# Where the preparation of a state-space layer stands among the matmuls: turns, powers and tables of eight blocks at other places

## The reference

```python
x = x + 0.5 * swiglu(rms_norm(x, g[0]), ffn_w_in[0, 0], ffn_w_out[0, 0])   # x @ w_in, silu(gate) * up, @ w_out
h = rms_norm(x, g[1])
lam_bar = jnp.exp(lam * step)
b_bar = ((lam_bar - 1.0) / lam)[..., None] * b
# x_t = lam_bar x_{t-1} + b_bar u_t,  y_t = Re(C x_t) + D u_t, by group
x = x + s5_mixer(h, ...)
```

## Time and profile before

| | |
|---|---|
| median of three runs | 1791.58 us (1790.89 to 1791.99) |
| profiled execution, its own time | 1792.96 us |
| its span, first to last instruction | 1791.1 us |
| mean granted clock of TensorE | 0.995 |
| TensorE busy | 1753.7 us, 98% of the span |
| VectorE, ScalarE, POOL busy | 928.5, 652.6, 324.7 us |

### The profile page before, as it was taken

One profiled execution on the slowest core, in us unless ns is written; L12 is line 12 of the kernel. 1 busy time (PEld: TensorE's weight loads), 2 busy tenths in 40 slices (PEclk: granted clock), 3 DMA queues, 4 the chain that ended last, 5 costly groups with the idle time before them and its releaser, 6 DMA issues.

```text
span 1791.1 us, 22436 instructions
## 1 busy us (share of the span) xinstructions
PE 1753.7 (98%) x8598; PEld 1435.5 (80%) x8598; DVE 928.5 (52%) x1067; ACT 652.6 (36%) x897; POOL 324.7 (18%) x276
## 2 busy tenths in 40 slices
PE   9999899997999999999999999999999999999998
PEld 6787787876788888888888888888777888888887
DVE  7768978648555344433374334333674544444333
ACT  6332233347434333332253333322474433333222
POOL 8997533016014000000000000000200200000000
PEclk9999999999999999999999999999999999999999
DMA  5364645588433332333223332333310333322321
GB/s 200 118 165 123 182 133 157 156 301 311 143 102 96 95 94 95 100 98 94 94 83 107 103 95 94 95 101 99 96 46 1 107 106 100 97 94 94 97 91 47
DMA packets 80788, 206.50 MB, mean 115 GB/s; under 512 B 24048, under 2 KB 34416, under 8 KB 79696
## 3 DMA queue, kind: packets, MB, share of 16 engines
q1 hardware_dynamic: 69664, 189.86, 33.6%
q0 software_dynamic: 2592, 13.51, 2.2%
q10 hardware_dynamic: 8464, 2.20, 0.5%
HBM read 182.46 MB, written 23.07 MB: 115 GB/s over the span
## 4 chain that ended last, share of the span: by engine, by line
PE 83%; DVE 6%; ACT 3%; POOL 3%; DMA 2%; issue 2%; ACTq 0%; SPq 0%; DVEq 0%; POOLq 0%
PE bank L1628 26%; PE bank L1630 26%; PE bank L1629 26%; DVE w_split L1179 2%; ACT w_split L761 1%; DMA op_slot<-s_ops 1%; PE bank L1979 1%; PE bank L1958 1%; ACT x_gained L792 0%; DVE ops_out L1228 0%; DVE up L1223 0%; ACTq L794 0%; DVE gate L1222 0%; DVE ops_out L1225 0%; DVE ops_out L1224 0%
## 5 line engine op out<-in xcount | busy, mean ns | idle before, releaser
L1179 DVE TENSOR_TENSOR w_split<-w_raw,w_split 128x1024 fp32r<-128x1024 f32 x296 | 402.9, 1365 | 624.4 <-ACT w_split L761 623.7
L1628 PE MATMUL bank<-h_split,w_split 128*128 128x512 f32 x1504 | 589.1, 392 | 2.4 <-DVE gate L1191 0.9
L1630 PE MATMUL bank<-h_split,w_split 128*128 128x512 f32 x1504 | 585.4, 389 | 0.0
L1629 PE MATMUL bank<-h_split,w_split 128*128 128x512 f32 x1504 | 585.2, 389 | 0.0
L761 ACT ACTIVATE w_split<-w_raw 128x1024 fp32r<-128x1024 f32 x296 | 312.2, 1058 | 642.5 <-PE bank L1630 634.2
L1628 PE MATMUL bank<-g_split,w_split 128*128 128x512 f32 (+1 forms) x854 | 330.4, 387 | 8.5 <-DVE w_split L1179 4.9
L1628 PEld LDWEIGHTS bank<-h_split,w_split 128*128 128x128 f32 x1504 | 282.3, 188 | 65.3 <-DVE h_split L1198 2.0
L1629 PEld LDWEIGHTS bank<-h_split,w_split 128*128 128x128 f32 x1504 | 282.4, 188 | 59.1 <-issue 1.2
L1630 PEld LDWEIGHTS bank<-h_split,w_split 128*128 128x128 f32 x1504 | 282.3, 188 | 58.9
L1629 PE MATMUL bank<-g_split,w_split 128*128 128x512 f32 (+1 forms) x854 | 329.3, 386 | 0.0
L1630 PE MATMUL bank<-g_split,w_split 128*128 128x512 f32 (+1 forms) x854 | 329.2, 385 | 0.0
(11 more groups left out here) (298 smaller groups left out, 1154.0 us busy)
## 6 DMA issues: line engine op xcount, KB each, us to landing
w_raw<-wstream SPq DMA_DIRECT2D x296, 512.0 KB, 3.5
op_slot<-s_ops SPq DMA_DIRECT2D x5, 2048.0 KB, 13.5
s_ops<-ops_out SPq DMA_DIRECT2D x16, 512.0 KB, 3.0
op_slot<-s_ops POOLq DMA_DIRECT2D x3, 2048.0 KB, 14.1
s_ops<-c_pow POOLq DMA_DIRECT2D x8, 512.0 KB, 5.2
s_ops<-k_window SPq DMA_DIRECT2D x64, 64.0 KB, 3.3
x_res<-xT SPq DMA_DIRECT2D x8, 256.0 KB, 6.2
s_u<-x_gained ACTq DMA_DIRECT2D x8, 256.0 KB, 7.6
```

The costliest lines, as they stand in the source:

```text
L1179: tt(W[:, r, 1, :], RAW[:, r, :], W[:, r, 0, :].bitcast(F32), ALU.subtract).then_inc(s_lo, 1)
L1628: mm(bank, hi, x_hi, start=start, stop=True, skip_group_check=True)
L1629: mm(bank, hi, x_lo, start=False, stop=True, skip_group_check=True)
L1630: return mm(bank, lo, x_hi, start=False, stop=True, skip_group_check=True)
```

## The change

Nothing is added or removed but waits: the same operations stand at other places. Turns: block 0 goes from input tile 4 to 5 of part one, 3 from output tile 2 to 3, 4 from output tile 5 of part one to input tile 1 of part two, 5 from input tile 2 to 3, 7 from 8 to 7; blocks 1, 2 and 6 stay. The taps follow one tile behind. Tables: blocks 0 and 1 go from output tiles 0 and 1 of part one to 2 and 5, block 2 from output tile 4 to input tile 0 of part two, 3 from input tile 1 to 3, 4 from 4 to 6, 5 from 6 to 7, 7 from 10 to 9; block 6 stays at 8. One wait is added on POOL: the powers of blocks 3 and later start when the low half of part one's last gate is written. Two calls of `s5_ops` are added, since none stood at input tiles 0 (VectorE) and 1 (TensorE).

```diff
--- before.py
+++ after.py
@@ -80,12 +80,12 @@
 
 IN, OUT = range(2)
 S5_STAGES = (FFN0A1, FFN0A2)
-TURN_AT = {(FFN0A1, IN, 4): 0, (FFN0A1, IN, 7): 1, (FFN0A1, IN, 9): 2, (FFN0A1, OUT, 2): 3, (FFN0A1, OUT, 5): 4,
-           (FFN0A2, IN, 2): 5, (FFN0A2, IN, 5): 6, (FFN0A2, IN, 8): 7}
-TAPS_AT = {(FFN0A1, IN, 5): 0, (FFN0A1, IN, 8): 1, (FFN0A1, IN, 10): 2, (FFN0A1, OUT, 3): 3, (FFN0A1, OUT, 6): 4,
-           (FFN0A2, IN, 3): 5, (FFN0A2, IN, 6): 6, (FFN0A2, IN, 9): 7}
-TABLES_AT = {(FFN0A1, OUT, 0): 0, (FFN0A1, OUT, 1): 1, (FFN0A1, OUT, 4): 2, (FFN0A2, IN, 1): 3, (FFN0A2, IN, 4): 4,
-             (FFN0A2, IN, 6): 5, (FFN0A2, IN, 8): 6, (FFN0A2, IN, 10): 7}
+TURN_AT = {(FFN0A1, IN, 5): 0, (FFN0A1, IN, 7): 1, (FFN0A1, IN, 9): 2, (FFN0A1, OUT, 3): 3, (FFN0A2, IN, 1): 4,
+           (FFN0A2, IN, 3): 5, (FFN0A2, IN, 5): 6, (FFN0A2, IN, 7): 7}
+TAPS_AT = {(FFN0A1, IN, 6): 0, (FFN0A1, IN, 8): 1, (FFN0A1, IN, 10): 2, (FFN0A1, OUT, 4): 3, (FFN0A2, IN, 2): 4,
+           (FFN0A2, IN, 4): 5, (FFN0A2, IN, 6): 6, (FFN0A2, IN, 8): 7}
+TABLES_AT = {(FFN0A1, OUT, 2): 0, (FFN0A1, OUT, 5): 1, (FFN0A2, IN, 0): 2, (FFN0A2, IN, 3): 3, (FFN0A2, IN, 6): 4,
+             (FFN0A2, IN, 7): 5, (FFN0A2, IN, 8): 6, (FFN0A2, IN, 9): 7}
 
 N_IN0A, N_S5, N_IN0B, N_KV, N_LAT, N_DQ, N_IN1B, N_FINAL = range(8)
 
@@ -652,6 +652,7 @@
             powers(tt, link, PA, 7, t1, t2)
             nc.gpsimd.memset(TM[:, 0:8], 0.0).then_inc(s_near, 1)
             pool.wait_ge(s_near, 1)
+            pool.wait_ge(s_g_lo, HALF)
             for k in range(3, BLOCKS):
                 make_powers(k)
 
@@ -1271,6 +1272,8 @@
                     dve.wait_ge(s_rstd, n + 1)
                 gated(stage, 0, 0, stage + 2)
                 split(stage, 3)
+                if stage == FFN0A2:
+                    s5_ops(stage, IN, 0)
                 ffn_in_loop(stage)
 
             def add_ffn(stage, d):
@@ -1726,6 +1729,8 @@
                 in_tile(stage, 1, 1, base, src, within=within)
                 if after:
                     after()
+                if stage == FFN0A2:
+                    s5_ops(stage, IN, 1)
                 if stage not in S5_STAGES:
                     in_turns(pe, stage, ffn_in_turn)
                     return
```

## The result

The changed kernel takes 1796.09 us (median of 17 runs, 1792.25 to 1796.67) against 1792.01 of the kernel before on the same chip (17 runs, 1789.62 to 1795.15): a ratio of 1.0015, 95% interval 1.0009 to 1.0022. It is slower by 2.7 us by the ratio (4.1 by the medians), where 1783 was forecast; both the range and the likeliest case are missed.

The account below looks back on a forecast made before the run. TensorE was taken as the bound (83% of the chain), its four waits and lowered clock costing 16.35 us; less new waits and clock of 1.0, 1.5, 3.3 and 1.8, 8.75 is gained: 1783 us, range 1776 to 1790.

Parts of the forecast that it names:

- Turn 0, and part one's last gate: Part one: TensorE's waits of 2.21 us ahead of turn 0 and 3.15 in output tile 0 go, with 1.8 of clock.
- Tables 0 beside powers 4: Part one's output tiles: tables 0 run wholly beside powers 4; the 4.91 us wait shrinks to 1.0 (0 to 2).
- The last gate of part two: First output tile of part two: a new wait of 3.3 us (1.9 to 5) for tile 10's gate, with 1.8 of clock.
- The next two iterations repeat what the trace shows: Part two, VectorE after turn 4: unchanged until iteration 3, which starts 26.7 us behind the end of input tile 1.
- TensorE wants them behind tiles 4 and 5 and turns 5 and 6: Part two: banks wanted 25.0 us after input tile 3, free at 26.2; a wait of 1.5 (0 to 4), without clock.
- Turn 1: Part one: POOL's step into block 1's c_pow may start some us later, and turn 1 has two tiles for it.
- The sum: Whole kernel: 16.35 - 1.0 - 1.5 - 3.3 - 1.8 = 8.75 us gained, 1784.2 for the profiled execution.
- The signs of being wrong: Tables 0 ending before 175, no operation of tables 3 held, or the last wait outside 1.9 to 5 us.
- the signs listed for the forecast: No wait at turn 0 or part one's first output tile; tables 0 at 12 us or more; gate waits 1.5 and 3.3.
- The case slower than before: Rival, part two: longer VectorE backlog makes the last gate 13.7 us late, with 5 of clock; 1796.5; 5%.
- Full blocking: Rival, part two: each POOL operation in iteration 3 holds VectorE for its whole length; a wait of 6 us; 1790; 18%.

Follow-up runs that it names:

- experiment 4: The changed kernel without POOL's added wait for part one's last gate: 1800.46 us, ratio 1.0058 to the kernel before.
- experiment 2: The changed kernel with part two's turns 4 to 7 at input tiles 1, 4, 7, 9, taps and tables moved to suit: 1789.23 us, ratio 0.9983 to the kernel before.
- experiment 10: The changed kernel with tables 3 at input tile 4 and tables 7 at input tile 10 of part two: 1782.55 us, ratio 0.9947 to the kernel before.
- experiment 9: The changed kernel with POOL's powers of blocks 5 to 7 done for the first channel group only: 1782.26 us, ratio 0.9941 to the kernel before.
- experiment 3: The changed kernel with tables 7 behind part two's last gate, at input tile 10 for 9: 1789.04 us, ratio 0.9991 to the kernel before.
- experiment 1: The changed kernel with ScalarE's copies of a turned block ahead of the next input tile's gate in part two: 1792.01 us, ratio 1.0004 to the kernel before.
- experiment 7: The kernel with turns three tiles apart in part two, with tables 0 moved to input tile 9 of part one: 1789.06 us, ratio 0.9978 to the kernel before.
- experiment 8: The changed kernel with SyncE's load of the last u ahead of operator loads 4 and 5: 1794.74 us, ratio 1.0013 to the kernel before.

## Why the prediction was wrong, step by step

- **Turn 0, and part one's last gate: right.** Both waits are gone and the clock is 1.00 there; experiment 4 brings the second back, and costs 7.7 us by the ratios and 5.3 by the medians, where 3.15 + 1.8 was the term.
- **Tables 0 beside powers 4: right in kind, the wait smaller.** They run from 168.51 to 184.5, 15.9 us (15.35 was taken). The low half behind them was forecast 1.0 us late (0 to 2); it was on time, while in experiments 2 and 10 it was 1.1 late.
- **The last gate of part two: right.** 3.3 us and 1.8 of clock were forecast, 2.98 and 1.9 came. Experiment 9 gives 3.00 with POOL all but silent, so it is the plain addition of VectorE's operations that the term was worked out as; experiment 3 removes it by moving the one set of tables.
- **"The next two iterations repeat what the trace shows": right, and it hid the failure.** Iteration 3 was to start 26.7 us behind turn 4's place and did at 27.2 (247.32); the banks were to be free 26.2 us behind turn 5 and were 26.9 (273.35, against turn 5's start at 246.49; that start was itself 2.94 late, so from the end of tile 3, the E3 of the prediction, it is 29.8). Experiment 1 shows the case that the prediction reckoned with, a turn 5 that does not wait: iteration 3 and tables 3 are held by 8.0 us where 8.1 was taken, the banks are free at E3 + 27.0, and TensorE waits 1.96 where 1.5 was taken. The stretch of VectorE's operations was thus sized well. Its rows in experiment 1, turn 5 on TensorE and then VectorE's iteration 3, tables 3 and the gate behind them:

```profile
243.75 0.63 PE L1707 MATMUL bank<-c_pow,b_pow 128*16 128x128 f32 x16
...
247.84 1.21 DVE L1183 TENSOR_TENSOR w_split<-w_raw,w_split 128x1024 fp32r<-128x1024 f32 x1
...
266.77 0.68 DVE L1232 TENSOR_TENSOR ops_out<-ops_out,up 128x512 f32<-128x512 f32 x1
...
270.01 0.69 DVE L1195 TENSOR_TENSOR gate<-gate,bank 128x512 f32<-128x512 f32 x1 [0.70 <-ACT gate L768]
```

  The step that failed is the one behind it: "TensorE wants them behind tiles 4 and 5 and turns 5 and 6". What TensorE wanted first was turn 6, and a turn waits for ScalarE's copies of the block before, 4 us further down ScalarE's order than the gate's second operation. For a turn the sum held no wait but POOL's. Where it had 1.5 us without clock, 2.94 + 6.25 came, with 4.4 of clock. A smaller miss lies beside it: no term had a gate wait behind powers 7, and experiment 1, where no turn of part two waits, has 3.16 us there.
- **It could be read before.** ScalarE's timeline before, behind turn 5 at 246.43, three tiles ahead of turn 6:

```profile
266.66 0.63 ACT L767 ACTIVATE gate<-gate 128x512 f32<-128x512 f32 x1 [6.50 <-DVE gate L1189]
268.58 1.04 ACT L761 ACTIVATE w_split<-w_raw 128x1024 fp32r<-128x1024 f32 x1
...
271.09 1.09 ACT L814 ACTIVATE ops_out<-bank 128x512 f32<-128x512 f32 x2
```

  The copies end at 272.18, 25.75 us behind the turn that they copy. Three tiles and a turn are 34.3 us, two are 23.37. Two tiles apart the next turn waits 2.4 us if VectorE is as late as it was here, beside powers 6, and not later; 2.94 came. With those powers cut to one group in eight the copies end by 22.5 (experiment 9), and nothing waits. For turn 6 the stretched tables stand ahead of that gate as well.
- **Turn 1: missed for the same reason.** Turn 0 moved from three tiles ahead of turn 1 to two, and 1.14 us of wait for the copies of block 0 came. All ten experiments leave this place as the change has it, and of the eleven profiled executions five have the wait, at 1.14 to 1.18 us, and six none: the margin is near zero.
- **The sum.** Forecast were 7.6 us of waits and clock left of 16.35; 19.6 are there. The difference, 12.0, is the gap between the forecast for the profiled execution, 1784.2, and its 1796.6, but for 0.4.
- **The signs of being wrong.** None of the three came true: tables 0 ended at 184.5, operations of tables 3 were held, and the last wait was 2.98. They tested the terms that the sum had, and none looked at a turn. Of the signs listed for the forecast only the wait of 1.5 us for a gate near input tile 6 is missing.
- **The rivals.** The case slower than before came out with its time (1796.5) and not with its mechanism, so that its time is luck: the last gate was to be late by 13.7 and was by 2.98. Full blocking (1790) put its 6 us on the same gate of part two as the forecast; its rule, that of the Trainium skill, "SBUF — State Buffer", section "SBUF: two separate sides", says that a VectorE operation with both inputs in SBUF and a POOL operation that reads SBUF shut each other out. The trace agrees in kind (3.3 and 3.6 us for operations of 1.1, and experiment 9's low halves of 1.232 against 1.610 mean), but not in the size that the rival drew from it: tables 3 took 12.1 us, with three of six operations held, and in experiment 1 iteration 3 and tables 3 together were held by the 8.0 us named above, where the rival took six times 2.2, or 13.2.

From the last addition of part two to the end experiments 2 and 7 seem to need 2 us less than the others (1389.3 and 1389.0, against 1390.3 to 1391.9). They do not: from the end of TensorE's matmuls of part two they need 1392.2 us, the others 1390.6 to 1392.2. In these two the last addition comes 2.92 and 3.24 us behind that, against 0.27 to 0.31 in all others, and TensorE's waits of 2.58 and 2.90 us for ScalarE's square stand there. Not settled is what makes VectorE late at that place.

## What to carry to other kernels

When an operation is moved nearer to its predecessor, list everything that it waits for, over all engines, and measure in the trace how long behind the predecessor each of these ends; the margin is the distance less that time, and here it was there to be read, 25.75 against 23.37 us. An engine that is late by some us costs nothing until TensorE comes to want its result. That moment comes sooner where unrelated work of a third engine is queued behind the wait for it, as the copies were behind the gate: look for such work. And look where the lateness is made before moving its waiters: reordering the copies alone shifted 9 us of waits to the gates, while moving one set of tables off powers 6 removed 6.25, of which 1.4 came back further on.

## What the runs showed of the hardware

- Waits of 2.94 and 2.98 us lowered the granted clock (0.91 in their windows), one of 3.16 at 285 in experiment 1 left it at 1.00: the length of a single wait does not decide it. After the wait of 6.25 TensorE lost 2.9 us more in the two tiles behind, without any wait. So equal sums of waits differ in time: part two of experiment 1 has 12.2 us of waits as the change has, and the last addition comes at 399.93 in place of 403.08.
- A store of 256 KB, issued at 406.30 behind three loads of 2 MB (the first at 403.0, two from 404.3), landed after 17.62 us, and after 7.0 when two of these loads came behind it (experiment 8).
